# The wide sum of each weight-block pair: two accumulating GpSimd transfers in place of one VectorE addition

## The chip, the cores and the metric

One NeuronCore of one Trainium2 chip runs the kernel. The metric is the device time of one execution in microseconds (us). TensorE (PE in the rows) multiplies, VectorE (DVE) and ScalarE (ACT) prepare its operands and take its results, GpSimd (POOL) issues some transfers, and SyncE (SP) issues the weight loads. All four of them meet at semaphores.

## What is computed

One layer of a streaming encoder on 640 tokens (512 of a prompt, 128 of running streams): a half-step feed-forward network, a mixer with two recurrent branches, and a second half-step feed-forward network. The change is in the two feed-forward networks alone:

```python
D_MODEL, FFN_DIM = 1024, 2816

def _swiglu(x, w_up, w_down):
    gate, up = jnp.split(x @ w_up, 2, axis=-1)
    return (jax.nn.silu(gate) * up) @ w_down

def _layer(x, ...):
    x = x + 0.5 * _swiglu(_rmsnorm(x, p['norm_ffn1_g']), p['ffn1_w_up'], p['ffn1_w_down'])
    mix, lcv, lh, scv, sh = _mixer(_rmsnorm(x, p['norm_mix_g']), ...)
    x = x + mix
    x = x + 0.5 * _swiglu(_rmsnorm(x, p['norm_ffn2_g']), p['ffn2_w_up'], p['ffn2_w_down'])
```

## The kernel before

Every fp32 product is made as three products of split operands: a weight block is cut into a rounded part (`w_hi`, by ScalarE) and the rest (`w_lo`, by VectorE, which subtracts the rounded part from the raw block), the activations likewise, and TensorE multiplies hi*hi, lo*hi and hi*lo.

The 22 column tiles of 128 of gate and up in each feed-forward network are worked in three groups of 8, 8 and 6. Group 0 (`PLAIN`) is made directly. In groups 1 and 2 a **pair**, the gate tile and the up tile of one column, is made by a scheme of seven half-size products in place of eight (`pair` on TensorE, `seven_pair` on ScalarE and VectorE). There are 8 + 6 pairs in each network, 28 in all, numbered m = 0 to 27; a **run** is the pairs of one group, so there are four runs (8, 6, 8, 6). Between runs stand the eight down-projection units of a group.

Of the raw weights of pair m four blocks of 128x512 are loaded by SP (line 435): G0 and G1, the two halves over the contraction of the gate tile, and U0 and U1 of the up tile. Even m use `w_raw`, odd m the free halves of `xq`. From them come four sums:

- the **wide sum**, one VectorE addition of 128x1024 (`add_blocks`, line 1997), writes both halves of `s_raw`: `sums(0)` = G0+U0 and `sums(1)` = U1+U0;
- S2 = `sums(1)`+G0 and S4 = S2+G1, two additions of 128x512 (lines 1998 and 1999), go to `squares`.

There is one `s_raw`, used by every pair in turn. `cut_s31` splits the wide sum (ScalarE line 1315, VectorE line 2018), `cut_s2` splits S2 (1305, 2007), `cut_w1` splits G0 and G1 (1310, 2012), `cut_s4` and `cut_w22` the rest (1320 and 2024, 1324 and 2029). All are counted in `st_hi` and `st_lo` by their place within a pair.

TensorE's seven products of a pair stand in the order Q1, Q5, Q6, Q2, Q7, Q3, Q4, of 12 matmuls each. Q1 waits for `cut_w1` of its pair, Q5, the second, for `cut_s31`, Q3 for `cut_s4`, Q4 for `cut_w22`. The sums and most cuts of pair m+1 are made while TensorE works on pair m, so that they lie one pair ahead; for the first pair of a run they are made beside the last two down-projection units (the end of `ffn` on VectorE and ScalarE). Each engine's order is written out by hand; an engine that waits holds up all that stands behind it on its queue.

GpSimd has nothing to do during the feed-forward networks: in the first it stands at line 573, a wait for the end of the network, and its last instruction before the second has been issued when that begins.

## Time and profile before

| | us |
|---|---|
| median of three runs (1798.34 to 1799.03) | 1798.42 |
| the profiled execution | 1798.24 |
| its span, first to last instruction | 1796.3 |
| TensorE busy | 1778.2 (99%) |
| VectorE busy | 1261.4 (70%) |
| ScalarE busy | 758.5 (42%) |
| GpSimd busy | 130.1 (7%) |

The profile shows one execution. Busy time of an engine says how much work it has; what a change is worth depends on who waits for whom, which the lists of waits and the rows in order of time show. 1.94 us of the profiled execution lie outside the span.

### The profile page before, as it was taken

What the parts mean: (1) busy time and instruction counts of PE and PEld (TensorE: products, weight loads), DVE (VectorE), ACT (ScalarE), POOL (GpSimd) and SP (SyncE); (2) the same over time, 40 slices, a digit from 0 to 9 for tenths busy, and PEclk for the clock granted to TensorE, in tenths of its full rate; (3) what the DMA queues carried; (4) which work ended last, traced back from release to release, by engine and by line L of the source; (5) the groups of instructions that cost most, each with busy time, mean ns of one, the idle gap of its engine ahead of it and who ended that gap; (6) DMA issues with size and microseconds to landing.
All of it is one profiled execution on the core that took longest, in us unless ns stands there. A gap on an engine that the chain in (4) does not pass through costs nothing.

```text
span 1796.3 us, 30145 instructions
## 1 busy us (share of the span) xinstructions
PE 1778.2 (99%) x12265; PEld 1731.2 (96%) x12265; DVE 1261.4 (70%) x1610; ACT 758.5 (42%) x1091; POOL 130.1 (7%) x258
## 2 busy tenths in 40 slices
PE   8999999999999999999999999999999999999998
PEld 8999999999999999989989989999999999999998
DVE  6665784586787875787788887877855765862864
ACT  5322553254577752244245245234332332541544
POOL 4000000000012120111101011100200000000000
PEclk9999999999999999999999999999999999999999
DMA  5222322331322253353444335346622223322322
GB/s 154 70 70 64 112 72 79 86 88 53 132 80 68 76 143 115 113 173 92 124 127 141 102 95 175 119 123 204 210 77 71 70 77 87 95 71 75 90 64 89
DMA packets 274023, 185.42 MB, mean 103 GB/s; under 512 B 8236, under 2 KB 261364, under 8 KB 273664
## 3 DMA queue, kind: packets, MB, share of 16 engines
q1 hardware_dynamic: 240880, 129.52, 25.0%
q0 software_dynamic: 10240, 35.86, 6.3%
q10 hardware_dynamic: 22800, 18.62, 3.2%
q8 instruction: 71, 1.16, 0.3%
q14 instruction: 32, 0.26, 0.0%
HBM read 161.43 MB, written 22.53 MB: 102 GB/s over the span
## 4 chain that ended last, share of the span: by engine, by line
PE 87%; DVE 8%; ACT 3%; issue 2%; DMA 0%; SPq 0%; ACTq 0%; DVEq 0%
PE pu L732 59%; PE pu L801 10%; PE pn L801 10%; DVE w_lo L1787 2%; DVE squares L1781 1%; PE pn L1031 1%; ACT w_hi L1182 1%; PE pn L924 1%; PE pn L1054 1%; PE pn L1073 1%; PE pn L1048 1%; PE pn L1020 0%; PE pu L1103 0%; DVE t_raw L1781 0%; PE pn L1085 0%
## 5 line engine op out<-in xcount | busy, mean ns | idle before, releaser
L732 PE MATMUL pu<-act_hi,w_hi 128*128 128x320 f32 x1940 | 452.6, 314 | 0.8 <-DVE xc L1781 0.4
L732 PE MATMUL pu<-act_lo,w_hi 128*128 128x320 f32 x1940 | 442.7, 309 | 0.0
L732 PE MATMUL pu<-act_hi,w_lo 128*128 128x320 f32 x1940 | 442.4, 309 | 0.0
L1787 DVE TENSOR_TENSOR w_lo<-w_raw,w_hi 128x1024 fp32r<-128x1024 f32 x184 | 225.3, 1224 | 217.7 <-ACT w_hi L1182 216.0
L732 PEld LDWEIGHTS pu<-act_hi,w_hi 128*128 128x128 f32 x1940 | 323.8, 188 | 14.2 <-issue 11.7
L732 PEld LDWEIGHTS pu<-act_lo,w_hi 128*128 128x128 f32 x1940 | 325.0, 188 | 0.9 <-DVE act_lo L1832 0.7
L732 PEld LDWEIGHTS pu<-act_hi,w_lo 128*128 128x128 f32 x1940 | 325.2, 188 | 0.0
L1182 ACT ACTIVATE w_hi<-w_raw 128x1024 fp32r<-128x1024 f32 x184 | 194.0, 1054 | 247.2 <-PE pu L732 233.6
L732 PE MATMUL pu<-x_hi,w_hi 128*128 128x320 f32 x544 | 125.2, 311 | 4.2 <-DVE ff_g L1848 3.2
L732 PE MATMUL pu<-x_hi,w_lo 128*128 128x320 f32 x544 | 124.1, 309 | 0.0
L732 PE MATMUL pu<-x_lo,w_hi 128*128 128x320 f32 x544 | 124.0, 309 | 0.0
L732 PEld LDWEIGHTS pu<-x_hi,w_hi 128*128 128x128 f32 x544 | 90.8, 188 | 6.4 <-DVE ff_g L1848 4.3
L732 PEld LDWEIGHTS pu<-x_lo,w_hi 128*128 128x128 f32 x544 | 91.0, 188 | 0.0
L732 PEld LDWEIGHTS pu<-x_hi,w_lo 128*128 128x128 f32 x544 | 91.0, 188 | 0.0
L1626 ACT ACTIVATE lmat<-lmat 128x1024 f32<-128x1024 f32 x20 | 21.2, 1060 | 135.2 <-DVE lmat L2426 135.2
L732 PE MATMUL pu<-yn_hi,w_hi 128*128 128x320 f32 x256 | 62.4, 325 | 0.1
L732 PE MATMUL pu<-yn_lo,w_hi 128*128 128x320 f32 x256 | 58.3, 309 | 0.0
L732 PE MATMUL pu<-yn_hi,w_lo 128*128 128x320 f32 x256 | 58.2, 309 | 0.0
L801 PE MATMUL pu<-x_hi,w_hi 128*128 128x320 f32 x168 | 52.1, 310 | 0.2 <-DVE w_lo L2012 0.2
L801 PE MATMUL pu<-t_hi,s_hi 128*128 128x320 f32 x168 | 52.2, 311 | 0.0
L801 PE MATMUL pn<-t_hi,s_hi 128*128 128x320 f32 x168 | 52.0, 310 | 0.0
L801 PE MATMUL pn<-x_lo,w_hi 128*128 128x320 f32 x168 | 51.9, 309 | 0.0
(432 smaller groups left out, 3394.2 us busy)
## 6 DMA issues: line engine op xcount, KB each, us to landing
w_raw<-in_w_in_dram SPq DMA_DIRECT2D x73, 512.0 KB, 3.7
w_raw<-in_ffn_w_down_dram SPq DMA_DIRECT2D x32, 512.0 KB, 3.6
w_raw<-in_ffn_w_up_dram SPq DMA_DIRECT2D x31, 512.0 KB, 3.7
w_raw<-in_ffn_w_up_dram SPq DMA_DIRECT2D x56, 256.0 KB, 3.8
xq<-in_ffn_w_up_dram SPq DMA_DIRECT2D x56, 256.0 KB, 4.0
da_rep<-e_spill POOLq DMA_DIRECT2D x20, 512.0 KB, 4.0
w_raw<-in_w_br_ssd_dram SPq DMA_DIRECT2D x16, 512.0 KB, 3.5
w_raw<-in_ffn_w_down_dram SPq DMA_DIRECT2D x16, 384.0 KB, 3.2
```

The costliest lines, as they stand in the source:

```text
L732: ins = pe.matmul(dst[:, h, :], w[:, side, c, :], a[:, k, h * HALF:(h + 1) * HALF], start=(at == 0), stop=(at == n - 1))
L801: ins = pe.matmul(dst, w(k), a(k), start=start and k == 0 and w is hi and a is b_hi, stop=stop and k == KH - 1 and a is b_lo, skip_group_c ...
L924: ins = pe.matmul(pn[w][:, h, 0:HALF], w_gates[:, w, :], xc[:, h * HALF:(h + 1) * HALF], start=True, stop=True)
L1031: ins = pe.matmul(pn[0][r:r + HD, 0, (h // 2) * P:(h // 2 + 1) * P], xd[:, h, :], lmat[:, h, :], start=True, stop=True)
L1048: ins = pe.matmul(pn[0][:, 1, q * P:(q + 1) * P], ht[:, 2 * q:2 * q + 2, :].rearrange("n a b -> n (a b)"), xft(g, 5)[:, t * P:(t + 1) * P] ...
L1054: pe.matmul(pn[1][:, 1, :], b_tok[:, :], xdd[:, :, :].rearrange("p h d -> p (h d)"), start=True, stop=True).then_inc(s["ssd_p"], 1)
L1073: ins = pe.transpose(pn[1][:, b // 4, (b % 4) * P:(b % 4 + 1) * P], h0[qq][:, a, b, :], ident[:, :])
L1182: act.activation(w_hi[:, side, :, :], w_raw[:, side, :, :], ACT.Copy).then_inc(s["w_hi_done"], 1)
L1626: act.activation(lmat[:, :, :], lmat[:, :, :], ACT.Exp).then_inc(s["ssd_a"], 1)
L1781: return dve.scalar_tensor_tensor(out=dst, in0=a, scalar=scalar, in1=b, op0=op0, op1=op1)
L1787: dve.tensor_tensor(w_lo[:, side, :, :], w_raw[:, side, :, :], w_hi[:, side, :, :].bitcast(F32), ALU.subtract).then_inc(s["w_lo_done"], 1)
```

## The change

The wide sum is no longer made by VectorE. SP loads G0 and U1 a second time, straight into the two halves of `s_raw` (two transfers of 256 KB, semaphore `st_part`), and GpSimd, when both have landed, issues two transfers that add U0, read from DRAM again, onto each half (`accum_op=ALU.add`, 256 KB each, semaphore `st_whole`; the new function `whole_sums`). `s_raw` is written again only when `cut_s31` of the pair before has been done by VectorE, for which SP waits. The waits of `cut_s31` on ScalarE and of `add_blocks` on VectorE go to `st_whole`. `whole_sums(0)` stands on GpSimd's queue ahead of its first wait for the mixer, `whole_sums(1)` at its end.

Beside this the order within a pair changes: on VectorE `cut_w1(m+1)` now stands ahead of `add_blocks(m+1)`, and `cut_s2(m+1)` moves from there to the end, between the second addition to a PSUM bank (line 2069 before) and `cut_s31(m+1)`; on ScalarE `cut_s2(m+1)` moves from ahead of `cut_w1(m+1)` to behind the copy of `up1`.

```diff
@@ -44,11 +44,11 @@
-Q_PER, C_PER, SUM_PER, CUT_PER, U_PER = 7, 4, 3, 5, 2
+Q_PER, C_PER, SUM_PER, CUT_PER, U_PER = 7, 4, 2, 5, 2
-SUM_A, SUM_S2, SUM_S4 = range(1, 4)
-CUT_S2, CUT_W1, CUT_S31, CUT_S4, CUT_W22 = range(1, 6)
+SUM_S2, SUM_S4 = 1, 2
+CUT_W1, CUT_S2, CUT_S31, CUT_S4, CUT_W22 = range(1, 6)
@@ -433,6 +433,12 @@
                                 sp.dma_start(dst, cols(w_up, c, k0, KH)).then_inc(s[f"st_in{m % 2}"], 16)
+                            if m in (0, RUN_AT[1, 1]):
+                                sp.wait_ge(s["rs_step"], 4 * (GROUPS + 2) + 4 if m else 4)
+                            else:
+                                sp.wait_ge(s["st_lo"], CUT_PER * (m - 1) + CUT_S31)
+                            for j, (c, k0) in enumerate(((gate, 0), (up, KH))):
+                                sp.dma_start(sums(j), cols(w_up, c, k0, KH)).then_inc(s["st_part"], 16)
                         sp.wait_ge(s["st_lo"], CUT_PER * (run + n - 2) + CUT_W22)
@@ -569,6 +575,19 @@
+            def whole_sums(f):
+
+                w_up = (ffn1_w_up[0], ffn2_w_up[0])[f]
+                for gi in (1, 2):
+                    for i in range(FFN_GROUPS[gi]):
+                        m = RUN_AT[f, gi] + i
+                        at = FFN + (sum(FFN_GROUPS[:gi]) + i) * P
+                        pool.wait_ge(s["st_part"], 32 * (m + 1))
+                        for j in range(2):
+                            pool.dma_start(sums(j), w_up[0:KH * P, at:at + P].rearrange("(k p) c -> p k c", p=P),
+                                           accum_op=ALU.add).then_inc(s["st_whole"], 16)
+
+            whole_sums(0)
             pool.wait_ge(s["out_free"], O_DT)
@@ -710,6 +729,7 @@
             pool.wait_ge(s["tails_out"], 16 * TAIL_DMAS)
+            whole_sums(1)
@@ -1271,9 +1291,9 @@
                         m = run_of(u, gi + 1)
-                        cut_s2(m)
                         down(KT // 2 - 1, 0, False)
                         cut_w1(m)
+                        cut_s2(m)
                         cut_s31(m)
@@ -1311,7 +1331,7 @@
-                act.wait_ge(s["st_sum"], SUM_PER * m + SUM_A)
+                act.wait_ge(s["st_whole"], 32 * (m + 1))
                 act.activation(s_hi[:, 0:2, :, :].rearrange("p s k c -> p s (k c)"), s_raw[:, :, 0:KH * P], ACT.Copy).then_inc(s["st_hi"], 1)
@@ -1349,12 +1369,12 @@
                 else:
-                    cut_s2(m + 1)
                     q(Q2)
...
                 if not end:
+                    cut_s2(m + 1)
                     cut_s31(m + 1)
@@ -1953,9 +1973,9 @@
                         add_blocks(m)
-                        cut_s2(m)
                         down(KT // 2 - 1, 0, False)
                         cut_w1(m)
+                        cut_s2(m)
                         cut_s31(m)
@@ -1993,8 +2013,7 @@
                     dve.wait_ge(s["st_lo"], CUT_PER * (m - 1) + CUT_S4)
-                pair_sums = s_raw[:, :, 0:KH * P].rearrange("p s (k c) -> p s k c", k=KH)
-                chained("st_sum", base, dve.tensor_tensor(pair_sums, both, w2[:, 1:2].to_broadcast([P, 2, KH, P]), ALU.add), SUM_A)
+                dve.wait_ge(s["st_whole"], 32 * (m + 1))
                 chained("st_sum", base, dve.tensor_tensor(more_sums(0), sums(1), w1[:, 0], ALU.add), SUM_S2)
@@ -2059,15 +2078,15 @@
                 else:
+                    cut_w1(m + 1)
                     add_blocks(m + 1)
-                    cut_s2(m + 1)
-                    cut_w1(m + 1)
                 dve.wait_ge(s["st_c"], C_PER * m + C_UP1)
...
                 if not end:
+                    cut_s2(m + 1)
                     cut_s31(m + 1)
```

VectorE, pair m = 1 (the `pn` banks) of the first network, before; `s_raw` holds the wide sum, the two rows that write `squares` are S2 and S4, `s_lo<-squares` is `cut_s2`, `w_lo<-w_raw` 128x1024 is `cut_w1`, `s_lo<-s_raw` is `cut_s31`:

```order
L2029 TENSOR_TENSOR w_lo<-xq,w_hi 128x512 [waits st_hi]
L1997 TENSOR_TENSOR s_raw<-w_raw 128x2x512 [waits st_lo,st_in0]
L1998 TENSOR_TENSOR squares<-s_raw,w_raw 128x512 [waits st_sum]
L1999 TENSOR_TENSOR squares<-squares,w_raw 128x512 [waits st_sum]
L2007 TENSOR_TENSOR s_lo<-squares,s_hi 128x512 [waits st_hi]
L2012 TENSOR_TENSOR w_lo<-w_raw,w_hi 128x1024 [waits st_hi]
L2067 TENSOR_TENSOR pn<-pn,ff_g 128x320 [waits st_c]
L2069 TENSOR_TENSOR pn<-pn,ff_g 128x320 [waits st_q]
L2018 TENSOR_TENSOR s_lo<-s_raw,s_hi 128x1024 [waits st_hi]
L1781 SCALAR_TENSOR_TENSOR ff_a<-ff_t,pn 128x640 [waits ff_s,ff_th]
```

The same place after:

```order
L2048 TENSOR_TENSOR w_lo<-xq,w_hi 128x512 [waits st_hi]
L2031 TENSOR_TENSOR w_lo<-w_raw,w_hi 128x1024 [waits st_hi]
L2017 TENSOR_TENSOR squares<-s_raw,w_raw 128x512 [waits st_whole,st_lo,st_in0]
L2018 TENSOR_TENSOR squares<-squares,w_raw 128x512 [waits st_sum]
L2085 TENSOR_TENSOR pn<-pn,ff_g 128x320 [waits st_c]
L2087 TENSOR_TENSOR pn<-pn,ff_g 128x320 [waits st_q]
L2026 TENSOR_TENSOR s_lo<-squares,s_hi 128x512 [waits st_hi]
L2037 TENSOR_TENSOR s_lo<-s_raw,s_hi 128x1024 [waits st_hi]
L1801 SCALAR_TENSOR_TENSOR ff_a<-ff_t,pn 128x640 [waits ff_s,ff_th]
```

The wide sum is gone, the narrow sums S2 and S4 stand behind `cut_w1` and wait for `st_whole`, and `cut_s2` stands behind both additions to the PSUM banks.

VectorE, the end of the down-projection units ahead of a run (here pair 0), before; the rows that write `resid` take the last two units' results:

```order
L1997 TENSOR_TENSOR s_raw<-w_raw 128x2x512 [waits bn_lo,st_in0]
L1998 TENSOR_TENSOR squares<-s_raw,w_raw 128x512 [waits st_sum]
L1999 TENSOR_TENSOR squares<-squares,w_raw 128x512 [waits st_sum]
L2007 TENSOR_TENSOR s_lo<-squares,s_hi 128x512 [waits st_hi]
L1781 SCALAR_TENSOR_TENSOR resid<-pu,resid 128x640 [waits out_ready]
L2012 TENSOR_TENSOR w_lo<-w_raw,w_hi 128x1024 [waits st_hi]
L2018 TENSOR_TENSOR s_lo<-s_raw,s_hi 128x1024 [waits st_hi]
```

The same place after:

```order
L2017 TENSOR_TENSOR squares<-s_raw,w_raw 128x512 [waits st_whole,bn_lo,st_in0]
L2018 TENSOR_TENSOR squares<-squares,w_raw 128x512 [waits st_sum]
L1801 SCALAR_TENSOR_TENSOR resid<-pu,resid 128x640 [waits out_ready]
L2031 TENSOR_TENSOR w_lo<-w_raw,w_hi 128x1024 [waits st_hi]
L2026 TENSOR_TENSOR s_lo<-squares,s_hi 128x512 [waits st_hi]
L2037 TENSOR_TENSOR s_lo<-s_raw,s_hi 128x1024 [waits st_hi]
```

Here the narrow sums, with the wait for `st_whole`, have stayed ahead of the `resid` row and of `cut_w1`.

SP's queue from the loads of pair 0 to those of pair 2, after; before, the rows that write `s_raw` are not there:

```order
L435 DMA w_raw<-in_ffn_w_up_dram 128x4x128 [waits w_lo_done]
L435 DMA w_raw<-in_ffn_w_up_dram 128x4x128 x3
L441 DMA s_raw<-in_ffn_w_up_dram 128x4x128 [waits rs_step]
L441 DMA s_raw<-in_ffn_w_up_dram 128x4x128
L435 DMA xq<-in_ffn_w_up_dram 128x4x128 [waits out_ready]
L435 DMA xq<-in_ffn_w_up_dram 128x4x128 x3
L441 DMA s_raw<-in_ffn_w_up_dram 128x4x128 [waits st_lo]
L441 DMA s_raw<-in_ffn_w_up_dram 128x4x128
L435 DMA w_raw<-in_ffn_w_up_dram 128x4x128 [waits st_lo]
```

Each pair's two loads into `s_raw` stand behind its four raw loads and ahead of the next pair's, with a wait of their own.

## Rows read from the trace of the kernel before

**Rows 1.** The page: busy time of each engine, its share and instructions.
```profile
PE 1778.2 (99%) x12265; PEld 1731.2 (96%) x12265; DVE 1261.4 (70%) x1610; ACT 758.5 (42%) x1091; POOL 130.1 (7%) x258
```
**Rows 2.** Stretch of pair 1: its length, busy PE, PEld, DVE, ACT, POOL, clock, DMA share.
```profile
201.89:214.20 12.31, 12.31 (x87) 12.31 (x86) 10.12 (x15) 7.73 (x13) 0.00 (x0) 1.00 0.30 87
```
**Rows 3.** TensorE in order of time: start us, us; Q1 and Q5 of pair 1.
```profile
201.89 0.31 PE L801 MATMUL pn<-x_hi,w_hi 128*128 128x320 f32 x1
...
203.65 0.31 PE L801 MATMUL pn<-t_hi,s_hi 128*128 128x320 f32 x1
```
**Rows 4.** VectorE in order of time, pair 1: start us, us, idle before in brackets.
```profile
206.29 0.68 DVE L2029 TENSOR_TENSOR w_lo<-xq,w_hi 128x512 fp32r<-128x512 f32 x1
206.90 1.22 DVE L1997 TENSOR_TENSOR s_raw<-w_raw 128x1024 f32<-128x1024 f32 x1
208.15 0.69 DVE L1998 TENSOR_TENSOR squares<-s_raw,w_raw 128x512 f32<-128x512 f32 x1
208.88 0.69 DVE L1999 TENSOR_TENSOR squares<-squares,w_raw 128x512 f32<-128x512 f32 x1
209.54 0.69 DVE L2007 TENSOR_TENSOR s_lo<-squares,s_hi 128x512 fp32r<-128x512 f32 x1
210.49 1.23 DVE L2012 TENSOR_TENSOR w_lo<-w_raw,w_hi 128x1024 fp32r<-128x1024 f32 x1 [0.26 <-ACT w_hi L1310]
211.63 0.49 DVE L2067 TENSOR_TENSOR pn<-pn,ff_g 128x320 f32<-128x320 f32 x1
212.63 0.50 DVE L2069 TENSOR_TENSOR pn<-pn,ff_g 128x320 f32<-128x320 f32 x1 [0.51 <-PE pn L801]
213.04 1.21 DVE L2018 TENSOR_TENSOR s_lo<-s_raw,s_hi 128x1024 fp32r<-128x1024 f32 x1
```
**Rows 5.** One line's instructions, VectorE's wide sum, the 14 even pairs: ns min/median/max.
```profile
L1997 DVE TENSOR_TENSOR s_raw<-w_raw x14: 1217/1220/1227, 184.1 to 1708.9; 128x1024 f32<-128x1024 f32 x14
```
**Rows 6.** SP's raw loads, line 435: issue ns, then us from issue to landing.
```profile
L435 SPq DMA_DIRECT2D w_raw<-in_ffn_w_up_dram x56: 367/507/737, 177.5 to 1698.2; - x56
...
DMA to landing us min/median/max: 2.7/3.9/5.7
```
**Rows 7.** GpSimd's own transfers (POOLq), all of the trace: KB each, us to landing.
```profile
h_a<-in_state_ssd_h_dram POOLq DMA_DIRECT2D x8, 512.0 KB, 6.4
h_b<-in_state_ssd_h_dram POOLq DMA_DIRECT2D x8, 512.0 KB, 5.7
es<-e_spill POOLq DMA_DIRECT2D x32, 128.0 KB, 3.7
merged<-gate_spill POOLq DMA_DIRECT2D x8, 640.0 KB, 6.4
```
**Rows 8.** The loads `merged`, line 689, and the loads `es`, line 628: issue and landing.
```profile
L689 POOL DMA_DIRECT2D merged<-gate_spill x8: 528/528/556, 1242.8 to 1275.8; - x8
...
DMA to landing us min/median/max: 4.2/6.4/10.8
...
L628 POOL DMA_DIRECT2D es<-e_spill x32: 617/621/637, 671.9 to 1183.2; - x32
```
**Rows 9.** In order of time, the start of the first run: VectorE, SP, TensorE.
```profile
184.05 1.22 DVE L1997 TENSOR_TENSOR s_raw<-w_raw 128x1024 f32<-128x1024 f32 x1 [5.80 <-DMA w_raw<-in_ffn_w_up_dram]
...
187.31 0.82 DVE L1781 SCALAR_TENSOR_TENSOR resid<-pu,resid 128x640 f32<-128x640 f32 x1
188.04 1.22 DVE L2012 TENSOR_TENSOR w_lo<-w_raw,w_hi 128x1024 fp32r<-128x1024 f32 x1
...
177.54 2.03 SPq L435 DMA_DIRECT2D w_raw<-in_ffn_w_up_dram  x4
179.61 3.44 SPq L435 DMA_DIRECT2D xq<-in_ffn_w_up_dram  x4
...
189.37 0.36 PE L801 MATMUL pu<-x_hi,w_hi 128*128 128x320 f32 x1
```
**Rows 10.** The list of waits: who waited for whom, us in total, times, longest.
```profile
DVE s_raw L1997 <- DMA w_raw<-in_ffn_w_up_dram: 22.4, 4, 6.0
```

More of the change, by code:

```diff
@@ L160 @@
 h0_in0 h0_in1 hs_step old_mm old_cp c_split fs_mm fs_cp ns_mm ns_v hs_out0 hs_out1 hp_mm hp_cp hp_out yz yn_hi_done yn_lo_done br_s gl_th gl_mul gl_out0 gl_out1 gl_in gl_next gl_last gs_add gs_out
-tn_x tn_t tn_v tn_hi tn_lo bn_v bn_hi bn_lo st_in0 st_in1 st_sum st_hi st_lo st_q st_c st_u
+tn_x tn_t tn_v tn_hi tn_lo bn_v bn_hi bn_lo st_in0 st_in1 st_part st_whole st_sum st_hi st_lo st_q st_c st_u
 ma_in0 ma_in1 ma_in2 ma_in3 mg_b mg_v mh_done ml_done reload tail_mm tail_cp tails_out fin_half fin_r fin_sq fin_add fin_g fin_sum fin_a fin_v y_a y_v y_dma""".split()
```

## The prediction, made before the changed kernel had run

> **What bounds the kernel now.** I began with the page's busy times: TensorE is busy for 1778.2 of 1796.3 us, VectorE for 1261.4 [rows 1]. Less work for VectorE can then give back at most the small waits of TensorE, while anything new that TensorE waits for costs its full length. Next I read one pair in detail. A pair lasts 12.3 us, TensorE is busy through all of it, VectorE for 10.1 us [rows 2]. Each of the seven products takes 1.76 us, the distance from Q1 at 201.89 to Q5 at 203.65 [rows 3]. The order in time of VectorE shows which of its results is nearest to being late: the low part of the wide sum for pair 2 ends at 213.04 + 1.21 = 214.25 [rows 4], and Q5 of pair 2 wants it at 201.89 + 12.3 + 1.76 = 215.95. So the slack is 1.7 us. At the start of a run the low part of G0 and G1 ends at 188.04 + 1.22 = 189.26 and Q1 begins at 189.37 [rows 9]: no slack at all. Those are the two places where the change acts, so the sum is made there.
>
> **What is removed.** 28 additions of 1.22 us [rows 5], 34 us of VectorE's time. In a pair VectorE has 2.2 us to spare anyway and TensorE none [rows 2], so I cost the gain at nothing. The sums were TensorE's cover for nothing else; the moves of cut_s2 and cut_w1 alone change an order on an engine with time to spare. They shift the end of the wide sum's low part from 214.25 to about 213.04 + 0.61 + 1.21 = 214.9 (cut_s2, 128x512, takes 0.61 us from its start to the next one's, as the like row at 206.29 does [rows 4]); Q5 still finds it 1.1 us early.
>
> **What is added, and the loop it closes.** There is one s_raw. The two part loads of a pair may go only when cut_s31 of the pair before is done on VectorE, the two accumulating transfers only when those loads have landed, the narrow sums only when the accumulations have landed, and cut_s31, which frees s_raw for the next pair, stands on VectorE behind the narrow sums. This is a ring that is walked once for every pair, and none of it can run ahead. TensorE's pair takes 12.3 us; if the ring takes longer, the ring sets the pace, and TensorE waits at Q5. Its length, from the end of one cut_s31 to the next:
>
> 1. Part loads. Two issues on SP of at least 0.37 us, the second landing 2.7 us after its issue at best, 3.9 us in the middle [rows 6]. Nothing else is on the DMA engines then (the four raw loads of the next pair wait for cut_w22, which ends at 206.97 while the last cut_s31 ended near the pair's start [rows 4]), so I take it near the best: 0.4 + 2.9 = 3.3 us. A semaphore's way to GpSimd adds 0.1.
> 2. The two accumulating transfers, call it A, from the first issue to the last landing. No row shows one. From below: plain transfers of GpSimd, 128 KB each, are issued in 0.62 us [rows 8] and land 3.7 us after it; 512 KB ones land after 5.7 to 6.4 us [rows 7]. Our two carry 512 KB together, so a plain pair would lie between 0.6 + 3.7 = 4.3 and 6.4, about 5.3 us. From above: an accumulation must read what is there as well as what is added and then write, and it starts when the raw loads of the next pair, 1 MB, are about to fill the same engines (DMA is busy for 0.30 of a 12.3 us pair [rows 2], 3.7 us). The longest landing of a queue of loads in this trace is 10.8 us (merged, 640 KB [rows 8]). Between 5.3 and 10.8 I take 8.0 us: one more pass over the data than a plain 512 KB load and a share of the raw loads in its way. It is a guess between bounds, and the whole forecast hangs on it.
> 3. VectorE from there to the end of cut_s31: the narrow sums 209.54 - 208.15 = 1.39 us, two additions to the PSUM banks of 0.41 us each (213.04 - 212.63), cut_s2 0.61, cut_s31 1.21: 4.0 us [rows 4]. ScalarE's copies of S2 and the wide sum run beside this.
>
> Together 3.3 + 0.1 + A + 4.0 = A + 7.4 us, so 15.4 us for A = 8.0, 3.1 us more than the pair. Runs of 8, 6, 8 and 6 pairs have 7 + 5 + 7 + 5 = 24 such steps: 24 x 3.1 = 74 us. The 1.1 us of slack doesn't soften this, since the run starts late already, as follows.
>
> **The start of a run.** VectorE keeps the narrow sums, now with the wait for the accumulations, ahead of the result of the last down unit but one and of cut_w1, for which Q1 waits. The raw loads of pair 0 are issued from 177.54 on and VectorE has them at 184.05 [rows 9]. The part loads are issued behind them, and land some 1.5 us later (half as many bytes again), at 185.6. The whole sums are there at 185.6 + A = 193.6; narrow sums 1.4, the resid row 0.73 (188.04 - 187.31 [rows 9]), cut_w1 1.22: Q1 can begin at 197.0 in place of 189.3, 7.7 us late (A - 0.3). There are four such starts; all four show the same wait for the raw loads now [rows 10]. 4 x 7.7 = 31 us. The waits that SP gains stand ahead of loads which wait for a later event anyway (cut_w22), and GpSimd's queue holds nothing else that is due in a feed-forward network: nothing for these.
>
> **Sum.** 74 + 31 = 105 us, on the profiled execution's own 1798.24: 1903 us. That execution lies 0.18 us under the median, which changes nothing. In terms of A: 24 x (A - 4.9) + 4 x (A - 0.3). With A = 5.3 it is 10 + 20 = 30 us (1828), with 10.8 it is 142 + 42 = 184 us (1982).
>
> The state loads of 512 KB land in 5.7 and 6.4 us [rows 7]. The Trainium skill (DMA: Bandwidth & Descriptors, section Anatomy of one DMA, SWDGE path) puts a GpSimd transfer at about 2.0 us plus its bytes over 436 GB/s, which is an estimate of 3.2 us for 512 KB; the trace does not agree. By that rule A would be 3.8 us with the issue, and the first rival below would hold.
>
> **The rivals.**
>
> - Short transfers. If A is under 4.9 us, the ring is shorter than a pair and only the starts cost. For it: 3.7 us of the small plain loads [rows 7]. Against: 512 KB, twice the reading, and the raw loads in the way. With A near 4 us: 4 x 3.7 = 15 us, 1813. Chance 0.12.
> - Slow accumulation. If the read of the old value and the write of the new one are worked piece by piece, in the 512 byte pieces that a block's rows are made of, A can be well above any plain transfer. For it: nothing in the trace is like it; against: nothing too. With A = 14 us: 24 x 9.1 + 4 x 13.7 = 273 us, 2071. Chance 0.16.
> - The clock falls in the new waits. The granted clock is 1.00 here, the 2.4 GHz level [rows 2], with TensorE never idle for long. With waits of 3 us in each pair and 8 us at starts it may drop to 1.2 GHz and come back later. If one product's time (1.76 us) doubles after each of the 28 waits, 49 us come on top: 1952. Chance 0.07. The Trainium skill (TensorE: Matmul & The Clock Gate, Part 1) says that the throttled state is the default and activity releases it; no row here shows a wait in mid-kernel after which one could see it.
> - Not slower: the whole sums arrive before VectorE is ready for them, at the starts too. The point from which this decides is A = 0.3 us there, and within 0.2% (3.6 us in all) about 1.2 us, while GpSimd's plain loads of 128 KB already need 3.7 [rows 7]. It would need the part loads to have landed far sooner than their place on SP's queue allows. If VectorE's 34 us then bought anything, it would be the few tenths in which TensorE waits: about 1797. Chance 0.04, three quarters of it for no change that can be told.
>
> **Chances and range.** The forecast itself, A between 5.3 and 10.8 with 8.0 in the middle, has 0.61. Slower by over 0.2% 0.96, within 0.2% 0.03, faster by over 0.2% 0.01; 0.2% is about what a measurement of this kernel can tell from no change. The range reaches from 1822 (A = 5.1, part of the short-transfer case) to 2040 (A = 12.9, or 11.1 with the fallen clock), and leaves out some 0.1 on either side.
>
> **What would show it.** The changed kernel's waits should have VectorE's narrow sum waiting for a DMA transfer into s_raw 28 times; TensorE's Q5 should wait for cut_s31's low part in 24 pairs, 3 us each, and Q1 for cut_w1 four times, 7 to 8 us. The span from one pair's Q1 to the next should be A + 7.4. GpSimd's rows should give A directly: two issues of about 0.6 us and a landing 7 us after the second. If the pair still takes 12.3 us and A is over 5, my ring is wrong; if Q1 of a run isn't late, the order at the start is; if both waits are there with another length, only A was missized.

## The result, and the profile of the changed kernel

The changed kernel takes 1964.8 us in the median (1964.27 to 1966.93, 4 runs), the kernel before 1798.4 us (1797.37 to 1799.03, 4 runs) beside it: a ratio of 1.0925, 95% interval 1.0911 to 1.0939. That is 166 us slower. The prediction had the sign, the mechanism and the range (1822 to 2040) right; its middle of 1903 us is 62 us short.

The page after: busy times, the granted clock in tenths over the span, the software queue's packets, MB and share, and the chain that ended last by engine.

```profile
PE 1830.8 (93%) x12265; PEld 1777.6 (91%) x12265; DVE 1224.7 (62%) x1582; ACT 754.6 (38%) x1091; POOL 202.9 (10%) x314
...
PEclk9999888988999999999999999999999998899999
...
q0 software_dynamic: 39808, 50.54, 11.9%
...
PE 62%; DMA 17%; DVE 12%; issue 4%; ACT 3%; POOL 1%; SPq 1%; DVEq 0%; ACTq 0%; POOLq 0%
```

VectorE has lost 28 instructions and 36.7 us against [rows 1], as meant. TensorE, with the same 12265 matmuls, is busy 52.6 us longer, and the DMA is now 17% of the chain. The profiled execution's span is 1963.7 us against 1796.3, so 167.4 us are to be found. The list of waits (who waited for whom, us in total, times, longest) names them:

```profile
DVE squares L2017 <- DMA s_raw<-in_ffn_w_up_dram: 162.9, 28, 14.6
...
PE pn L821 <- DVE s_lo L2037: 49.7, 14, 5.1
PE pu L821 <- DVE s_lo L2037: 39.4, 10, 5.7
PE pu L821 <- DVE w_lo L2031: 26.7, 4, 6.8
```

VectorE's narrow sum (`squares`) waits for a transfer into `s_raw` 28 times, TensorE's Q5 for `cut_s31` in 14 + 10 = 24 pairs (89.1 us), and its Q1 for `cut_w1` four times (26.7 us): the three waits that were forecast, with their counts. 89.1 + 26.7 = 115.8 us of waits and 52.6 us of longer busy time are 168.4, the whole difference within 1 us. (The two overlap a little: the modelled end of a matmul lies beyond the start of the next, so that a wait in the list is some tenths shorter than the time it costs, and the rest stands in the busy time.)

One turn of the ring, in order of time over three engines (start us, us, idle before in brackets), from the end of one `cut_s31` to the next at L2037:

```profile
214.44 1.22 DVE L2037 TENSOR_TENSOR s_lo<-s_raw,s_hi 128x1024 fp32r<-128x1024 f32 x1
215.68 0.92 SPq L441 DMA_DIRECT2D s_raw<-in_ffn_w_up_dram  x2
215.71 0.64 PE L821 MATMUL pn<-t_hi,s_hi 128*128 128x320 f32 x1 [2.78 <-DVE s_lo L2037]
...
219.63 2.59 POOL L587 DMA_DIRECT2D s_raw<-in_ffn_w_up_dram  x2 [15.15 <-DMA s_raw<-in_ffn_w_up_dram]
...
220.56 2.71 SPq L435 DMA_DIRECT2D xq<-in_ffn_w_up_dram  x4
...
228.86 0.69 DVE L2017 TENSOR_TENSOR squares<-s_raw,w_raw 128x512 f32<-128x512 f32 x1 [3.89 <-DMA s_raw<-in_ffn_w_up_dram]
```

The cut ends at 215.66, SP issues the part loads at once, GpSimd has them 4.0 us later (219.63), VectorE the whole sums 9.2 us after that (228.86), and 3.95 us later the next cut is done. The raw loads of the pair after, 1 MB, go out at 220.56, 0.9 us behind GpSimd's first issue. This turn is an exception there: in the other 19 turns with such loads SP issues them 0.1 to 2.0 us ahead of it. Over the 24 turns these legs are on average: load 4.48 us, A (GpSimd's first issue to the narrow sum) 9.60 us, VectorE 3.95 us; the ring 18.03 us (16.0 to 20.2) against a pair of 12.31 us.

How long the two issues take and when they land (ns min/median/max of an issue; us from issue to landing), and the part loads likewise:

```profile
L587 POOL DMA_DIRECT2D s_raw<-in_ffn_w_up_dram x56: 1259/1321/1877, 185.8 to 1888.6; - x56
...
DMA to landing us min/median/max: 4.4/7.7/10.2
...
L441 SPq DMA_DIRECT2D s_raw<-in_ffn_w_up_dram x56: 367/506/1043, 179.5 to 1882.9; - x56
...
DMA to landing us min/median/max: 2.8/3.3/5.5
```

The start of the first run, beside [rows 9]:

```profile
177.40 2.03 SPq L435 DMA_DIRECT2D w_raw<-in_ffn_w_up_dram  x4
179.47 1.15 SPq L441 DMA_DIRECT2D s_raw<-in_ffn_w_up_dram  x2
180.67 3.99 SPq L435 DMA_DIRECT2D xq<-in_ffn_w_up_dram  x4
185.85 2.68 POOL L587 DMA_DIRECT2D s_raw<-in_ffn_w_up_dram  x2 [162.48 <-DMA s_raw<-in_ffn_w_up_dram]
...
192.72 0.69 DVE L2017 TENSOR_TENSOR squares<-s_raw,w_raw 128x512 f32<-128x512 f32 x1 [14.61 <-DMA s_raw<-in_ffn_w_up_dram]
...
194.79 1.22 DVE L2031 TENSOR_TENSOR w_lo<-w_raw,w_hi 128x1024 fp32r<-128x1024 f32 x1
...
196.06 0.64 PE L821 MATMUL pu<-x_hi,w_hi 128*128 128x320 f32 x1 [6.67 <-DVE w_lo L2031]
```

Q1 begins at 196.06 where it began at 189.37. Last, the stretches of busy time (length, PE, PEld, DVE, ACT, POOL, clock, DMA share, GB/s) of the first 3.3 us after that wait, of a whole turn of the ring (compare [rows 2]) and of its first 3 us:

```profile
196.06:199.40 3.34, 3.34 (x12) 3.34 (x13) 3.02 (x4) 0.00 (x0) 0.00 (x0) 0.50 0.09 25
215.70:232.90 17.20, 13.97 (x85) 13.71 (x85) 8.90 (x13) 7.67 (x14) 2.59 (x2) 0.90 0.59 123
...
215.71:218.70 2.99, 2.99 (x11) 2.99 (x12) 2.04 (x3) 1.51 (x4) 0.00 (x0) 0.50 0.59 174
```

After the wait the clock is granted at 0.50, the 1.2 GHz level: 12 matmuls take 3.34 us, where a product takes 1.76 us at 1.00 [rows 3]. Over the whole trace TensorE is busy for 102.6 us in stretches granted 0.50, and none before. At half the clock that is 51.3 us more for the same work, nearly all of the 52.6.

### The profile page after: what moved, and what is told of

Same layout as the page of the kernel before. It is cut to its first block, busy times and chain, and to the rows that moved or that the text cites. A ratio compares the mean times of both kernels' runs of the same rounds, so it can differ in the third digit from the quotient of the medians.

```text
span 1963.7 us, 30232 instructions
## 1 busy us (share of the span) xinstructions
PE 1830.8 (93%) x12265; PEld 1777.6 (91%) x12265; DVE 1224.7 (62%) x1582; ACT 754.6 (38%) x1091; POOL 202.9 (10%) x314
## 4 chain that ended last, share of the span: by engine, by line
PE 62%; DMA 17%; DVE 12%; issue 4%; ACT 3%; POOL 1%; SPq 1%; DVEq 0%; ACTq 0%; POOLq 0%
PE pu L752 52%; DMA s_raw<-in_ffn_w_up_dram 17%; PE pn L821 2%; DVE s_lo L2037 2%; DVE w_lo L1807 2%; POOL s_raw L587 1%; ACT w_hi L1202 1%; DVE squares L1801 1%; PE pn L1051 1%; DVE squares L2017 1%; DVE squares L2018 1%; PE pn L944 1%; PE pn L1074 1%; PE pn L1093 1%; PE pn L1068 1%
## 5 line engine op out<-in xcount | busy, mean ns | idle before, releaser
L587 POOL DMA_DIRECT2D s_raw<-in_ffn_w_up_dram x56 | 72.4, 1537 | 894.2 <-DMA s_raw<-in_ffn_w_up_dram 882.3
L821 PE MATMUL pn<-t_hi,s_hi 128*128 128x320 f32 x168 | 62.2, 370 | 49.7 <-DVE s_lo L2037 49.7
L821 PE MATMUL pu<-t_hi,s_hi 128*128 128x320 f32 x168 | 63.7, 379 | 39.4 <-DVE s_lo L2037 39.4
L821 PEld LDWEIGHTS pn<-t_hi,s_hi 128*128 128x128 f32 x168 | 38.6, 230 | 53.4 <-DVE s_lo L2037 53.4
L821 PE MATMUL pu<-x_hi,w_hi 128*128 128x320 f32 x168 | 55.1, 328 | 26.7 <-DVE w_lo L2031 26.7
L1325 ACT ACTIVATE s_hi<-squares 128x512 fp32r<-128x512 f32 x28 | 17.6, 630 | 159.7 <-DVE squares L2017 159.7
L821 PEld LDWEIGHTS pu<-t_hi,s_hi 128*128 128x128 f32 x168 | 40.9, 243 | 42.0 <-DVE s_lo L2037 42.0
L2017 DVE TENSOR_TENSOR squares<-s_raw,w_raw 128x512 f32<-128x512 f32 x14 | 9.7, 692 | 103.9 <-DMA s_raw<-in_ffn_w_up_dram 103.9
```

What stands on the lines that cost most here:

```text
L587: pool.dma_start(sums(j), w_up[0:KH * P, at:at + P].rearrange("(k p) c -> p k c", p=P), accum_op=ALU.add).then_inc(s["st_whole"], 16)
L821: ins = pe.matmul(dst, w(k), a(k), start=start and k == 0 and w is hi and a is b_hi, stop=stop and k == KH - 1 and a is b_lo, skip_group_c ...
L2017: chained("st_sum", base, dve.tensor_tensor(more_sums(0), sums(1), w1[:, 0], ALU.add), SUM_S2)
```

## The experiments

Each is an edit of the changed kernel and was timed against the kernel before on the same chip (1798.2 to 1798.8 us). The means of a ring's legs are taken from the trace of each run, over its 24 turns. The question behind the first two is whether the moves cost anything; behind the next five, what the ring is made of; behind the last four, whether ring and starts are the whole cost.

### The moves alone

`e1_order_only` and `e1b_order_wide_first` have no part loads and no accumulations: VectorE makes the wide sum again, and only the moves of `cut_w1` and `cut_s2` stay. In the first the wide sum stands at the head of `add_blocks`, so behind `cut_w1`; in the second it stands ahead of `cut_w1`, where it was. The first, then what the second adds:

```diff
-                dve.wait_ge(s["st_whole"], 32 * (m + 1))
+                pair_sums = s_raw[:, :, 0:KH * P].rearrange("p s (k c) -> p s k c", k=KH)
+                chained("st_sum", base, dve.tensor_tensor(pair_sums, both, w2[:, 1:2].to_broadcast([P, 2, KH, P]), ALU.add), SUM_A)
```

```diff
                 else:
+                    wide_sum(m + 1)
                     cut_w1(m + 1)
                     add_blocks(m + 1)
```

> VectorE makes the wide sum again, no part loads and no accumulating transfers; only the moves within a pair stay (cut_w1 ahead of the sums, cut_s2 ahead of cut_s31). Theory of the ring (s_raw's chain of part loads, accumulations, narrow sums and cut_s31 sets the pace): the moves cost nothing, 1798 us, within 0.2% of before, Q5 never waits. Rival (a part of the loss is the order: cut_s2 and the wide sum's cut now end too late): Q5 waits for cut_s31 by some tenths of a us in each pair, 3 to 15 us more than before.

Measured 1816.5 us, ratio 1.0101 (1.0084 to 1.0118): 18 us where nothing was expected, and three beyond the most that its rival allowed. The list of waits and the order in time show why:

```profile
PE pn L813 <- DVE s_lo L2030: 7.0, 14, 0.5
PE pu L813 <- DVE s_lo L2030: 5.0, 10, 0.5
```

```profile
214.84 1.22 DVE L2030 TENSOR_TENSOR s_lo<-s_raw,s_hi 128x1024 fp32r<-128x1024 f32 x1
...
221.69 1.06 ACT L1322 ACTIVATE w_hi<-xq 128x1024 fp32r<-128x1024 f32 x1 [1.32 <-PE pu L813]
...
222.78 1.23 DVE L2024 TENSOR_TENSOR w_lo<-xq,w_hi 128x1024 fp32r<-128x1024 f32 x1 [2.85 <-ACT w_hi L1322]
...
223.92 1.22 DVE L2009 TENSOR_TENSOR s_raw<-xq 128x1024 f32<-128x1024 f32 x1
```

Q5 waits for `cut_s31` in all 24 pairs. `cut_w1` on VectorE waits for ScalarE's half, that one for TensorE's products after Q5; put behind it, the wide sum closes a ring through TensorE. The next `cut_s31` starts at 227.91, 13.07 us after this one, the length of nearly every turn of this trace, and 24 x (13.07 - 12.31) = 18 us, which is what was measured. (The list gives 12.0 us of waits: each of 0.50 us holds Q5 up by 0.77.)

> As the run before with the order alone (1816.5 us: every pair took 13.07 us, since cut_w1 waits on ScalarE for Q2 of the pair, and wide sum, narrow sums, two bank additions, cut_s2 and cut_s31 all stood behind it), but VectorE makes the wide sum ahead of cut_w1, where it had stood; only the moves that the changed kernel makes to the other instructions are left. The chain from one Q5 over Q2, cut_w1 and the rest to the next cut_s31 is then 13.07 - 1.25 = 11.8 us, under the pair's 12.3: if that chain explains the 18 us, 1798 us within 0.2%. If anything else in the moves costs, some us are left, 1802 or more.

Measured 1797.9 us, ratio 0.9997 (0.9988 to 1.0006, 11 runs). The moves are free; the 18 us belonged to the place of the wide sum in the first experiment, which the changed kernel doesn't have.

### What an accumulation costs beside a plain transfer

```diff
-                            pool.dma_start(sums(j), w_up[0:KH * P, at:at + P].rearrange("(k p) c -> p k c", p=P),
-                                           accum_op=ALU.add).then_inc(s["st_whole"], 16)
+                            pool.dma_start(sums(j), w_up[0:KH * P, at:at + P].rearrange("(k p) c -> p k c", p=P)).then_inc(s["st_whole"], 16)
```

> GpSimd's two transfers of each pair overwrite instead of accumulate: same bytes from DRAM, same queue, same waits; the sum lacks its first addend. In the changed kernel A (first issue to narrow sum) was 9.6 us in the mean. If the accumulation itself is the dear part (a read and a write of the old value for each piece): A falls to 5 to 6 us, the ring from 18.0 to about 14, 24 steps: 1965 - 4 x 24 = about 1870 us. If the raw loads in its way or GpSimd's issue of 1.3 us each are the dear part: A stays at 8.5 to 9.5 us and the time at 1940 to 1965.

Measured 1891.0 us (2 runs, 1886.8 and 1895.1; the trace is of the second), ratio 1.0514 (1.0487 to 1.0541).

```profile
L587 POOL DMA_DIRECT2D s_raw<-in_ffn_w_up_dram x56: 747/747/792, 185.3 to 1820.4; - x56
...
DMA to landing us min/median/max: 3.4/5.0/7.3
```

A falls from 9.60 to 6.82 us, the ring from 18.03 to 15.31; load and VectorE's part stay (4.55, 3.95). The time lies between the two expectations, nearer to the first. Accumulation costs 2.8 us of A: two plain issues take 1.49 us in place of 2.59, and the landing is the rest. More than half of the slowdown, 93 us, comes with plain transfers too.

### The raw loads in the way

From the third pair of a run on, the raw loads bring a quarter of their bytes. These pairs are worked with old weights.

```diff
+                                nk = KH if i < 2 else 1
-                                sp.dma_start(dst, cols(w_up, c, k0, KH)).then_inc(s[f"st_in{m % 2}"], 16)
+                                sp.dma_start(dst[:, 0:nk], cols(w_up, c, k0, nk)).then_inc(s[f"st_in{m % 2}"], 16)
```

> From the third pair of each run on, the four raw loads bring one 128x128 piece each instead of four, a quarter of the bytes (these pairs are worked with old weights). If A is long because 1 MB of raw loads runs on the same DMA engines: A falls from 9.6 to about 6.7 us, as at the starts of runs, the ring to about 15 us, 1965 - 20 x 3 = about 1905 us. If accumulating is slow by itself: A stays at 9 to 10 us, 1960 us or more.

Measured 1912.0 us (2 runs), ratio 1.0631 (1.061 to 1.0652). A is 7.21 us, the ring 15.67: the raw loads cost the accumulations 2.4 us. Their landing:

```profile
L588 POOL DMA_DIRECT2D s_raw<-in_ffn_w_up_dram x56: 1259/1322/1880, 186.3 to 1834.9; - x56
...
DMA to landing us min/median/max: 4.3/5.4/7.6
```

`e9_plain_light` makes both edits, to see whether these are two costs or one.

> Overwriting transfers as in the plain run (A 6.8 us, 2.8 less) and raw loads of a quarter as in the light run (A 7.2 us, 2.4 less) together; the output lacks the addends and from the third pair of a run on the weights are old. If the work of accumulating and the raw loads in the way are two separate costs: A about 4.4 us, ring 12.9, 24 x 0.6 + 4 x 5 on 1798: about 1832 us. If they are the same cost seen twice (an accumulation is dear only because it queues longer): A about 6 us, ring 14.4, about 1868 us.

Measured 1857.1 us (2 runs), ratio 1.0325 (1.0306 to 1.0343); A 5.30 us, ring 13.73. That is between the two expectations: 25 us over the first, 11 us under the second. If the two costs added up in full, A would be 9.60 - 2.78 - 2.39 = 4.4; if the one held the other, 6.8. Of the 5.2 us that they add up to, 4.3 are saved: they are mostly separate, with an overlap of 0.9 us.

### Half the bytes

Only `sums(1)` is made by transfers, VectorE adds G0+U0 (128x512) ahead of its wait.

```diff
-                            for j, (c, k0) in enumerate(((gate, 0), (up, KH))):
-                                sp.dma_start(sums(j), cols(w_up, c, k0, KH)).then_inc(s["st_part"], 16)
+                            sp.dma_start(sums(1), cols(w_up, up, KH, KH)).then_inc(s["st_part"], 16)
...
+                dve.tensor_tensor(sums(0), w1[:, 0], w2[:, 1], ALU.add).then_inc(s["st_sum"], 1)
+                dve.wait_ge(s["st_whole"], 16 * (m + 1))
```

> Everything is computed. Only the second half of the wide sum, U1+U0, is made by transfers: one part load of 256 KB and one accumulating transfer of 256 KB for each pair. The first half, G0+U0, is one VectorE addition of 128x512 (0.69 us), ahead of the wait for the transfer, so it is no part of the ring. Theory (an accumulation costs by its bytes and by GpSimd's issue): half the bytes and one issue of 1.3 us less, so A falls from 9.6 to about 6 us, the load leg from 4.5 to about 4.0; ring 14.0 us, 24 x 1.7 = 41 us, starts 4 x 3.5 = 14 us: about 1853. Rival (A is mostly a fixed delay of an accumulating transfer, or the wait behind the raw loads, whatever its size): A stays at 8 to 8.5 us, ring about 16.2: 24 x 3.9 = 94 us, starts 4 x 5.5 = 22 us: about 1914.

Measured 1858.1 us, ratio 1.0327 (1.031 to 1.0344), 5 us from the first theory. Load 3.51 us, A 6.61, ring 14.07; at the starts A is 4.8.

```profile
L585 POOL DMA_DIRECT2D s_raw<-in_ffn_w_up_dram x28: 1262/1282/1354, 185.2 to 1778.5; - x28
...
DMA to landing us min/median/max: 4.5/6.1/8.6
```

The second accumulating transfer of a pair costs 3.0 us, 1.3 of them its issue; the first costs 6.6. The pair leaves A 12.31 - 3.95 - 3.51 = 4.85 us, and even one transfer is over that.

### The order at the end of the ring

On VectorE `cut_s31` stands directly behind the S2 sum, ahead of S4, the bank additions and `cut_s2`; on ScalarE, and at the starts, it goes ahead of `cut_s2` too. TensorE waits for `cut_s2` at Q6 by itself.

```diff
                 chained("st_sum", base, dve.tensor_tensor(more_sums(0), sums(1), w1[:, 0], ALU.add), SUM_S2)
+                if between:
+                    between()
...
-                    add_blocks(m + 1)
+                    add_blocks(m + 1, lambda: cut_s31(m + 1))
```

> VectorE's cut_s31 directly behind the S2 sum, ahead of S4, the two bank additions and cut_s2 (and ScalarE's before its cut_s2; TensorE waits for cut_s2 at Q6). The transfers are untouched. Theory of the ring: its VectorE part falls from 3.95 to about 2.3 us, each of 24 steps by 1.65 us: 1965 - 40 = 1925 us. If the transfers alone set the pace and VectorE's share is not in the ring: no change.

Measured 1893.8 us, ratio 1.0524 (1.0508 to 1.054): 71 us back where 40 were expected. The same turn, first in the changed kernel, then here:

```profile
236.71 2.02 SPq L435 DMA_DIRECT2D w_raw<-in_ffn_w_up_dram  x4
237.03 2.60 POOL L587 DMA_DIRECT2D s_raw<-in_ffn_w_up_dram  x2 [14.81 <-DMA s_raw<-in_ffn_w_up_dram]
```

```profile
226.99 0.92 SPq L441 DMA_DIRECT2D s_raw<-in_ffn_w_up_dram  x2
...
231.15 2.59 POOL L587 DMA_DIRECT2D s_raw<-in_ffn_w_up_dram  x2 [11.19 <-DMA s_raw<-in_ffn_w_up_dram]
...
233.14 2.35 SPq L435 DMA_DIRECT2D w_raw<-in_ffn_w_up_dram  x4
```

VectorE's part fell from 3.95 to 2.27 us as expected. But the raw loads now come 2.0 us behind GpSimd's first issue (231.15, 233.14), where they came 0.3 us ahead of it (237.03, 236.71); in the median over the turns it is 2.05 us behind against 0.33 ahead. Load and A fell too, to 4.13 and 8.71: 24 x (18.03 - 15.11) = 70 us. That A fell because of the later raw loads is likely from `e5_light_raw`, but was not tested apart; why the load leg fell isn't shown (with the light raw loads it stayed). In a ring a gain in one leg also moves the others in time.

### The start of a run

Two tries. `e4_start_order` lets the narrow sums stand behind the `resid` row and `cut_w1` at the starts:

```diff
                         m = run_of(u, gi + 1)
-                        add_blocks(m)
                         down(KT // 2 - 1, 0, False)
                         cut_w1(m)
+                        add_blocks(m)
                         cut_s2(m)
```

> At the start of each run the narrow sums, with the wait for the accumulations, stand behind the resid row and cut_w1 on VectorE. Theory of the ring: Q1 no longer waits, Q5 does, for cut_s31, which now ends 0.73 + 1.22 us earlier after the whole sums; the run is earlier by 1.9 us, 4 x 1.9 = 7.5 us: 1957 us. Rival (Q1's wait at a start is beside the point, the transfers alone set the end): no change, 1965 us; or the 6.7 us of the four waits fall away wholly: 1938 us.

Measured 1954.9 us, ratio 1.0867 (1.0849 to 1.0885). 10 us come back, 7.5 were expected. The row of TensorE's waits that takes the place of the four at Q1:

```profile
PE pu L821 <- DVE resid L1801: 24.6, 4, 6.4
```

Q1 no longer waits, but Q5, 1.76 us behind it, does, 6.2 us on average. The profile names the last unit's `resid` row, which stands behind `cut_s31`; in the first run `cut_s31` ends at 196.25, that row at 196.99 and Q5 begins at 197.13, and both stand behind the late sums (192.69). From Q5 to Q5 the two traces differ by 7.0 us at the starts; the rest of the gain is in the ring (17.81 us in place of 18.03).

`e8a_early_parts` issues the part loads of a run's first pair ahead of the wait for the last down weights instead. `load_parts` is the change's own wait and two loads, as a function, called there (and at its old place for the other pairs):

```diff
+                            gate, up = (tile0 + i) * P, FFN + (tile0 + i) * P
+
+                            def load_parts():
...
+                                load_parts()
...
+                            if i:
+                                load_parts()
```

> Everything is computed. Like the changed kernel, but at the four starts of a run SP issues the two part loads of the first pair ahead of its wait for the last down weights and the raw loads, some 7 us or more earlier. Theory (Q1 of a run is late by A because the part loads stand behind the raw loads, and the ring inside a run isn't touched by that): the whole sums are there before VectorE asks for them, Q1 starts on time, 4 x 6.7 = 27 us come back, ring as before 18.0: about 1938. Rival (the accumulation is started earlier but then shares the DMA engines with the weights of the down projection and with the raw loads, so that it is late all the same, or these become late): under 10 us come back, 1955 to 1965.

Measured 1933.4 us, ratio 1.0752 (1.0734 to 1.077): 31 us back, 27 of waits and the slow clock behind them.

```profile
PE pn L829 <- DVE s_lo L2045: 51.9, 14, 6.3
PE pu L829 <- DVE s_lo L2045: 37.1, 10, 4.6
...
DVE squares L2025 <- DMA w_raw<-in_ffn_w_up_dram: 23.2, 4, 6.3
```

TensorE's four waits for `cut_w1` are gone; VectorE waits for the raw loads at the starts as it did before the change [rows 10]; the ring's 89.0 us of Q5 are what they were.

### Two buffers

In the second network the odd pairs' wide sum goes to other buffers that are free there (`rstd` and `tail`), so that the transfers of a pair wait for the `cut_s31` of the pair before the last. The first network has no room for that and is as changed. The core of it:

```diff
-                                sp.wait_ge(s["st_lo"], CUT_PER * (m - 1) + CUT_S31)
+                                sp.wait_ge(s["st_lo"], CUT_PER * (m - 2) + CUT_S31)
```

> In the second network alone odd pairs use another place for the wide sum, so that the part loads of a pair wait for the cut_s31 of the pair before the last. The first network stays as in the changed kernel. Theory of the ring: the ring no longer closes within a pair there; its 12 steps fall from 18.0 to 12.3 us, 1965 - 12 x 5.7 = about 1896 us, while the starts of runs stay 6.7 us late. Rival (the DMA engines or GpSimd's queue are the limit, with 2 MB read per pair and the additions): the pair stays at 14 us or more, 1915 us or more.

Measured 1899.8 us, ratio 1.056 (1.0544 to 1.0576).

```profile
PE pu L842 <- DVE w_lo L2056: 29.5, 4, 8.4
PE pn L842 <- DVE s_lo L2066: 24.3, 7, 6.2
PE pu L842 <- DVE s_lo L2066: 19.3, 5, 4.6
```

Q5 waits 12 times, once for every turn of the first network's ring, and once more, for 1.0 us, in the second. From Q5 to Q5 the second network's 12 turns take 2.3 us more than before, where the first network's take 64. The four late starts are still there. `e8_early_two_buffers` adds the early part loads at all four starts.

> Everything is computed. First network as in the changed kernel, with the early part loads at its two starts; second network with two buffers for the wide sum in turn and the early part loads at its two starts. Theory (ring and late start are the whole cost, and there is nothing else): the second network costs nothing against the kernel before, the first one its 12 ring steps of 5.7 us, 68 us: 1798 + 68 = 1866, with a few us for the first product after a wait at the slower clock about 1870. Rival (the accumulating transfers cost TensorE something beside waits, by the DMA engines or by ports to SBUF, or the early part loads don't help): the second network stays 15 us or more over its time in the kernel before, 1885 or more.

Measured 1866.4 us, ratio 1.038 (1.0355 to 1.0405). The sum was 1866 (12 x 5.7 us over the kernel before). The busy times of the last 406 us of its span, and the same stretch of the kernel before:

```profile
1460.00:1866.00 406.00, 396.69 (x2709) 394.90 (x2707) 235.66 (x318) 161.71 (x241) 36.09 (x28) 1.00 0.50 116
```

```profile
1390.00:1796.00 406.00, 397.90 (x2721) 396.64 (x2719) 255.77 (x328) 162.85 (x234) 0.00 (x0) 1.00 0.27 79
```

With the 28 transfers of GpSimd in it, and the DMA share nearly doubled, TensorE runs at a clock of 1.00 and nearly as before: from the second network's first Q5 to the end of the span it is 283.4 us against 281.9. The 1.5 us are lost in the last three turns of the third run (12.73, 12.72 and 13.48 us in place of 12.30), where VectorE's narrow sum waits for its accumulations again (0.8 to 1.5 us); in the fourth run, of 6 pairs, every turn takes 12.30. GpSimd's issues in that third run are 12.5 to 13.4 us apart, longer than a pair, so they fall behind turn by turn; whether a longer run would cost more, no experiment shows. VectorE has 20 us less to do in this stretch, and nothing comes of it. So the added DMA work costs TensorE next to nothing in itself; the ring and the late start are the cost.

The legs of the ring side by side, means over its 24 turns in us:

| | load | A | VectorE | ring | time |
|---|---|---|---|---|---|
| changed kernel | 4.48 | 9.60 | 3.95 | 18.03 | 1964.8 |
| `e6_cut_first` | 4.13 | 8.71 | 2.27 | 15.11 | 1893.8 |
| `e5_light_raw` | 4.52 | 7.21 | 3.95 | 15.67 | 1912.0 |
| `e2_plain` | 4.55 | 6.82 | 3.95 | 15.31 | 1891.0 |
| `e7_half_dma` | 3.51 | 6.61 | 3.95 | 14.07 | 1858.1 |
| `e9_plain_light` | 4.48 | 5.30 | 3.95 | 13.73 | 1857.1 |

In each row 24 x (ring - 12.31) and the waits of TensorE at the four starts (16 to 28 us) make the time over 1798.3 us, within 6 us.

## Why the prediction was right, and where its size failed

- **What bounds the kernel.** Right. TensorE is the bound, VectorE's 34 us are worth nothing: with ring and starts out of the way the second network of `e8_early_two_buffers` takes 1.5 us longer than before, not less.
- **The moves at nothing.** Right, by `e1b_order_wide_first` (0.9997). The reason given was too short: "an engine with time to spare" would have priced `e1_order_only` at nothing too, and its order costs 18 us by a ring through TensorE.
- **The ring.** Right in form: 24 waits at Q5, 28 of the narrow sum, and the ring's length is the sum of its legs. That VectorE's leg is 3.95 us in every turn shows that nothing of TensorE's is in it. Wrong in size by 2.6 us a turn, 15.4 against 18.03, 63 us in all:
  - *Part loads* 3.3 + 0.1 us, measured 4.48. The landing was taken near the best of [rows 6] and one issue for both. The two issues take 0.92 us, a landing 3.3 us in the median, and GpSimd waits for the later of the two. 1.1 x 24 = 26 us.
  - *A* 8.0 us, measured 9.60 (inside 5.3 to 10.8). The issue of an accumulating transfer was taken from plain ones at 0.62 us [rows 8] and is 1.3 us; the raw loads in the way, taken as "a share", cost 2.4 us. 1.6 x 24 = 38 us.
  - *VectorE* 4.0 us, measured 3.95.
- **The starts.** Right in place and count; A was 6.7 us there, not 8.0, so Q1 waited 6.7 us and not 7.7: 27 us in place of 31. The formula, 24 x (ring - 12.31) + 4 x the wait at Q1, gives 137 + 27 = 164 us with the measured legs; 167.4 were found. Measured from Q5 to Q5 in the two traces, the stretches with a start in them are 8.2, 10.7, 8.2 and 9.7 us longer, the turns between them 131.0 us, the end 0.3 us shorter. The two starts that stand behind another run of the same network are the dear ones, by 2.5 and 1.5 us: these would be the slow clock after the last wait of a run, where no ring hides it, and would make up for the other 3 us; no run had it alone.
- **Short transfers** did not come true: A was 6.4 us or more in every pair of the changed kernel, and a plain transfer of 256 KB lands after 5.0 us in the median and after 3.9 even with the light raw loads. But this rival was priced without its best row. [rows 7] are not all of GpSimd's transfers before; the page also has

```profile
da_rep<-e_spill POOLq DMA_DIRECT2D x20, 512.0 KB, 4.0
```

  20 loads of 512 KB that landed after 4.0 us in the median (3.7 to 5.9), where the prediction has 512 KB at 5.7 to 6.4 us. With its 0.6 us of issue a plain pair's lower bound would have been 4.6 us, under the 4.9 from which the ring costs. The Trainium skill (DMA: Bandwidth & Descriptors, section Anatomy of one DMA, SWDGE path) gives 2.0 us plus bytes over 436 GB/s, an estimate of 2.6 us for 256 KB; the shortest landing of GpSimd's into `s_raw` in any run took 3.4 us (`e2_plain`), so the traces do not agree.
- **Slow accumulation** did not come true: accumulating costs 2.8 us over plain (9.60 against 6.82), not a multiple of it.
- **The clock** did go down, as that rival said, and its price in TensorE's own time was near (49 us against 52.6 of longer busy time). But the rival put it on top of the ring, and that was the mistake: inside a run the ring is the longer chain, and a TensorE that is slower for two microseconds only waits less at the next Q5. Hence waits of 3.7 us a pair (89.1 / 24) where the ring is 5.7 us too long. The Trainium skill (TensorE: Matmul & The Clock Gate, Part 1) has the throttled state as the default that activity lifts; the rows agree: 0.50 right behind a wait of 6.67 us, 1.00 throughout in the stretch of `e8_early_two_buffers`, whose waits are under 1 us.
- **Not slower** did not come true: in the changed kernel no sum arrived ahead of its need. With two buffers most did.

The range of 1822 to 2040 came from A alone, and A was within its bounds. With A = 9.6 and a load leg of 4.5 us the ring's term would have been 24 x 5.8 = 139 us in place of 74, which is the miss. The load leg had no range of its own; its 26 us were covered only because A's range, a guess between bounds as the prediction says, was wide.

None of these kernels is faster than the one before, and the runs give no reason to look further: what was taken off VectorE was never on the path.

## What to carry to other kernels

Before moving work from an engine with slack to a DMA, draw the ring through the buffer that it fills: who frees it, who refills it, who reads it, and compare the sum of its legs with the time of one step. With one buffer every leg's latency is on the path; with two, and with the first loads issued ahead of unrelated ones, the same transfers cost 1.5 us in a network here, against some 83. And a change in order is priced by the chains that it closes, not by the engine's spare time.

## What the runs showed of the hardware

- An accumulating transfer from GpSimd is dearer to issue than a plain one of the same shape: two take 2.59 us against 1.49 (median 1.32 and 0.75 us apiece). For 256 KB in rows of 512 bytes it lands after 7.7 us in the median under this load, a plain one after 5.0.
- TensorE's clock after a wait of 6.7 us, and in the ring after one of 2.8 us, is at its 1.2 GHz level: the first matmuls at Q5 start 0.27 us apart, and 0.15 when the grant is back at 1.00. It is not so behind every wait: of the 28 in the changed kernel 20 were followed by a grant of 0.50 (0.54 behind one of them) over the first 1.5 us, and one of 2.95 us, at 421.3, by 1.00.
- Twice in the changed kernel GpSimd issued the second transfer of a pair 7 us after the first, and stood idle between them:

```profile
309.56 1.29 POOL L587 DMA_DIRECT2D s_raw<-in_ffn_w_up_dram  x1 [15.70 <-DMA s_raw<-in_ffn_w_up_dram]
316.85 1.28 POOL L587 DMA_DIRECT2D s_raw<-in_ffn_w_up_dram  x1 [6.00 <-issue]
```

  It is the sixteenth accumulating transfer of a network, in the eighth pair. The same place shows it wherever a network has two accumulations a pair into `s_raw` alone (with a gap of 4.7 to 9.0 us from issue to issue), in none with plain transfers, not with one transfer a pair, and not in the second network with two buffers. What it waits for the trace doesn't show, and no run was made for it; the two turns are 20.2 and 19.9 us long, and some 4 us of the 166 are theirs.
